# First head of the delta layer: key convolution in two halves, a hand-written inversion order, and the GpSimd remainders in four pieces

## The reference

```python
proj = hn @ w_in
qkv = jax.nn.silu(short_conv_centred(proj[..., :n_qkv], conv_w)).astype(f32)
gate = proj[..., n_qkv:n_qkv + B_VW].astype(f32)
ba = proj[..., n_qkv + B_VW:].astype(f32)
q = l2_norm(qkv[..., :B_KW].reshape(b, s, B_HEADS, B_HEAD_K))
...
beta = jax.nn.sigmoid(ba[..., :2 * B_HEADS]).reshape(b, s, 2, B_HEADS)
g = -jnp.exp(a_log.astype(f32)) * jax.nn.softplus(a + dt_bias.astype(f32))
o_fwd = gated_delta_chunked(q, k, v, g[:, :, 0], beta[:, :, 0])
o_bwd = flip(gated_delta_chunked(flip(q), flip(k), flip(v), flip(g[:, :, 1]), flip(beta[:, :, 1])))
...
# in gated_delta_chunked, per chunk and head:
lower = jnp.where(strict, jnp.einsum('bnhcd,bnhed->bnhce', kb, k) * decay, 0.0)
a_mat = jnp.eye(CHUNK, dtype=q.dtype) + lower
sol = lax.linalg.triangular_solve(a_mat, rhs, left_side=True, lower=True, unit_diagonal=True)
# then a scan over the chunks
```

## Time and profile before

| | |
|---|---|
| median of 3 runs | 1339.96 us (1338.75 to 1340.84) |
| profiled execution | 1342.17 us, span 1340.5 us |
| mean granted TensorE clock | 0.986 of full speed |
| busy: PE, PEld | 95%, 73% of the span |
| busy: DVE, ACT, POOL | 64%, 52%, 21% |
| chain that ended last | PE 75%, DVE 11%, ACT 9% |
| layer 0 and the passage to layer 1 | until about 517 us |
| first head's preparation and inversion | 517 to 628 us |

### The profile page before, as it was taken

One profiled execution on the slowest core, in us unless ns is written; L12 is line 12 of the kernel. 1 busy time (PEld: TensorE's weight loads), 2 busy tenths in 40 slices (PEclk: granted clock), 3 DMA queues, 4 the chain that ended last, 5 costly groups with the idle time before them and its releaser, 6 DMA issues.

```text
span 1340.5 us, 23647 instructions
## 1 busy us (share of the span) xinstructions
PE 1270.4 (95%) x8829; PEld 973.2 (73%) x8829; DVE 852.6 (64%) x2340; ACT 691.8 (52%) x1806; POOL 278.3 (21%) x188
## 2 busy tenths in 40 slices
PE   5999999999999999878999999999999999998997
PEld 4866766666667776667888888888888888865643
DVE  5334545444656545786897978879788797852343
ACT  6245465464564444535557485574856647552121
POOL 7220111020232244204104031040310403100000
PEclk9999999999999989888999999999999999999999
DMA  5111101011322231111011111110201101053111
GB/s 195 33 32 32 33 32 32 17 32 64 126 69 89 79 126 64 49 33 49 32 33 64 33 52 45 53 60 17 79 18 65 48 18 64 1 221 110 48 68 74
DMA packets 21761, 79.94 MB, mean 60 GB/s; under 512 B 3216, under 2 KB 3472, under 8 KB 20240
## 3 DMA queue, kind: packets, MB, share of 16 engines
q1 hardware_dynamic: 21648, 78.42, 17.0%
HBM read 63.66 MB, written 14.75 MB: 58 GB/s over the span
## 4 chain that ended last, share of the span: by engine, by line
PE 75%; DVE 11%; ACT 9%; issue 2%; DMA 2%; SPq 0%; POOL 0%; DVEq 0%; POOLq 0%
PE bank L1865 19%; PE bank L1765 17%; PE bank L1841 6%; PE bank L1905 4%; PE bank L1880 4%; PE bank L1792 4%; DVE arena L1504 3%; PE bank L1803 3%; PE bank L1818 3%; PE bank L1957 2%; PE bank L1964 2%; PE bank L1990 2%; PE bank L1938 2%; PE bank L1939 2%; PE bank L1950 2%
## 5 line engine op out<-in xcount | busy, mean ns | idle before, releaser
L1865 PE MATMUL bank<-hn_hi,w_hi 128*128 128x512 f32 x512 | 222.5, 435 | 0.5 <-ACT arena L1147 0.5
L1865 PE MATMUL bank<-hn_hi,w_lo 128*128 128x512 f32 x512 | 202.5, 395 | 0.0
L1865 PE MATMUL bank<-hn_lo,w_hi 128*128 128x512 f32 x512 | 201.4, 393 | 0.0
L1765 PE MATMUL bank<-hn_hi,w_hi 128*128 128x512 f32 x320 | 137.0, 428 | 0.5 <-ACT arena L1082 0.2
L1765 PE MATMUL bank<-hn_hi,w_lo 128*128 128x512 f32 x320 | 126.1, 394 | 0.0
L1765 PE MATMUL bank<-hn_lo,w_hi 128*128 128x512 f32 x320 | 125.8, 393 | 0.0
L1003 POOL TENSOR_TENSOR w_lo<-arena,w_hi 128x1024 fp32r<-128x1024 f32 x24 | 59.9, 2495 | 301.6 <-ACT w_hi L1178 301.6
L1113 ACT ACTIVATE arena<-bank 128x512 f32<-128x512 f32 x88 | 52.2, 598 | 118.0 <-PE bank L1803 118.0
L1865 PEld LDWEIGHTS bank<-hn_hi,w_lo 128*128 128x128 f32 x512 | 96.8, 189 | 22.1
L1363 DVE CUSTOM_DVE_ANT_0 arena<-bank,arena 128x384 f32<-128x384 f32 (+1 forms) x128 | 70.1, 581 | 63.7 <-issue 63.4
L1865 PEld LDWEIGHTS bank<-hn_hi,w_hi 128*128 128x128 f32 x512 | 97.6, 191 | 16.2 <-ACT arena L1147 0.7
(11 more groups left out here) (258 smaller groups left out, 2744.4 us busy)
## 6 DMA issues: line engine op xcount, KB each, us to landing
arena<-in_w SPq DMA_DIRECT2D x52, 512.0 KB, 3.5
arena<-in_x SPq DMA_DIRECT2D x16, 512.0 KB, 4.6
arena<-gc_scratch SPq DMA_DIRECT2D x8, 1024.0 KB, 4.8
x_scratch<-arena SPq DMA_DIRECT2D x13, 512.0 KB, 2.6
arena<-x_scratch SPq DMA_DIRECT2D x13, 512.0 KB, 3.5
out<-arena SPq DMA_DIRECT2D x8, 512.0 KB, 2.6
oT_scratch<-arena SPq DMA_DIRECT2D x7, 512.0 KB, 5.3
arena<-oT_scratch SPq DMA_DIRECT2D x7, 512.0 KB, 7.8
```

Of the source, the lines that this page charges most:

```text
L1765: ins = te.matmul(bank[r % 2][:], wp[:, tile % 2, k], hp[:, k, hf * HALF:(hf + 1) * HALF], start=(k == 0 and m == 0), stop=(k == KT - 1 an ...
L1865: ins = te.matmul(b[:], wp[:, t % 2, k], hp[:, k, hf * HALF:(hf + 1) * HALF], start=(k == 0 and m == 0), stop=(k == KT - 1 and m == 2))
```

## The change

The diff has six parts. (1) `first_inversion` replaces `inversion(0)`: the query's taps 0 and 1 before `x4`, 2 and 3 after `plain`, 4 after `y4`, then the value's five taps and SiLU (which stood before the inversion), then three taps of the next key, and its last two after `wqq`. (2) In front, eight items instead of four before the key's transposes, three instead of six before `subc`; one item more in all. (3) `lev` (level rows of the second direction, now with the zeroing of `invT`) stands right behind the first key's SiLU, not before `subc`; the zeroing left the place between the two copies of the gate logits. (4) The first key's half tiles are copied by ScalarE in front of and between its gate functions, and VectorE convolves tokens 0 to 509 before it builds its constants, the rest at the old place. (5) The second pair of the first head's four `subc` copies is VectorE's. (6) Every weight remainder at lines 955 and 1003 is made in four pieces of 256 columns; the semaphore rises after the last.

```diff
@@ -609,6 +609,39 @@
             def spread(h):
                 return [("init", h, rnd, p) for rnd in range(2) for p in range(2)] + [("turn", h)]
 
+            def first_inversion():
+
+                f(2)
+                conv("Q", 0, 0, 1)
+                f(1)
+                stage("x4", 0)
+                stage("plain", 0)
+                conv("Q", 0, 2, 3)
+                f(2)
+                stage("y4", 0)
+                conv("Q", 0, 4)
+                put(("silu", "Q", 0))
+                conv("V", 0, 0, 1, 2, 3, 4)
+                put(("silu", "V", 0))
+                f(2)
+                stage("x5", 0)
+                conv("K", 1, 0, 1, 2)
+                f(2)
+                put(("gramq", 0, 0), ("gramq", 0, 1))
+                stage("y5", 0)
+                put(("wqq", 0, 0, 0), ("wqq", 0, 0, 1), ("wqq", 0, 1, 0), ("wqq", 0, 1, 1))
+                conv("K", 1, 3, 4)
+                f(3)
+                stage("x6", 0)
+                f(2)
+                stage("y6", 0)
+                put(("root", 0))
+                f(2)
+                put(("vtr", 0, 0), ("vtr", 0, 1), ("silu", "K", 1))
+                f(4)
+                put(("tab1", 1), ("etm", 1, 0), ("etm", 1, 1))
+                f(3)
+
             def inversion(h):
                 prev, nxt = h - 1, h + 1
                 more = f if h < B_HEADS - 1 else fe
@@ -661,19 +694,17 @@
             put(("gcum",), ("gctr",))
             f(1)
             conv("K", 0, 0, 1, 2, 3, 4)
-            put(("silu", "K", 0), ("tab1", 0), ("etm", 0, 0), ("etm", 0, 1))
-            f(4)
+            put(("silu", "K", 0), ("lev",), ("tab1", 0), ("etm", 0, 0), ("etm", 0, 1))
+            f(8)
             put(("ktr", 0, 0), ("ktr", 0, 1), ("ssq", 0))
             f(4)
             put(("gramk", 0, 0), ("gramk", 0, 1), ("tabx", 0), ("ete", 0, 0), ("ete", 0, 1), ("stab", 0),
                 *[("wqk", 0, g, cc) for g in range(2) for cc in range(4)])
-            f(6)
-            put(("lev",), ("subc", 0, 0), ("subc", 0, 1), ("diag", 0, 0), ("diag", 0, 1), *sub_pieces(0))
+            f(3)
+            put(("subc", 0, 0), ("subc", 0, 1), ("diag", 0, 0), ("diag", 0, 1), *sub_pieces(0))
             f(25)
             put(*spread(0))
-            conv("V", 0, 0, 1, 2, 3, 4)
-            put(("silu", "V", 0))
-            inversion(0)
+            first_inversion()
             for h in range(1, B_HEADS):
 
                 sub = sub_pieces(h)
@@ -952,8 +983,11 @@
 
                     tile = e[1]
                     pool.wait_ge(w0_rounded, tile + 1)
-                    gp.tensor_tensor(w0_lo[:, tile % 2], ring0[:, tile % 2], w0_hi[:, tile % 2].bitcast(F32),
-                                     ALU.subtract).then_inc(w0_split, 1)
+                    for k in range(0, KT, 2):
+                        ks = slice(k, k + 2)
+                        ins = gp.tensor_tensor(w0_lo[:, tile % 2, ks], ring0[:, tile % 2, ks], w0_hi[:, tile % 2, ks].bitcast(F32),
+                                               ALU.subtract)
+                    ins.then_inc(w0_split, 1)
                 elif e[0] == "wosplit":
 
                     j = e[1]
@@ -1000,7 +1034,10 @@
                         continue
                     pool.wait_ge(w_rounded, t + 1)
                     pool.wait_ge(w_split, t)
-                    gp.tensor_tensor(w_lo[:, t % 2], ring1[:, t % 2], w_hi[:, t % 2].bitcast(F32), ALU.subtract).then_inc(w_split, 1)
+                    for k in range(0, KT, 2):
+                        ks = slice(k, k + 2)
+                        ins = gp.tensor_tensor(w_lo[:, t % 2, ks], ring1[:, t % 2, ks], w_hi[:, t % 2, ks].bitcast(F32), ALU.subtract)
+                    ins.then_inc(w_split, 1)
                 elif e[0] == "etm" and e[1] > 0:
 
                     h, d = e[1], e[2]
@@ -1117,6 +1154,14 @@
                     sc.activation(w_hi[:, i], ring1[:, i], ACT.Copy).then_inc(w_rounded, 1)
 
 
+            def first_key(hf):
+                e = ("proj", 0, hf, KT - 1)
+                act.wait_ge(W_full, W_DONE[w_key(e)])
+                sc.activation(raw[:, 0, 2 + hf * HALF:2 + (hf + 1) * HALF], w_bank(e)[:],
+                              ACT.Copy).then_inc(W_free[W_BANK[w_key(e)]], 1)
+
+            act.wait_ge(l1_ready, 1)
+            first_key(0)
             act.wait_ge(ba_tr, 1)
             act.wait_ge(ld_small, 16 * 7)
             bt = bank[4][:, 0:NT * 32].rearrange("p (c e) -> p c e", e=32)
@@ -1129,6 +1174,7 @@
             act.wait_ge(ba_dve, 2)
             sc.activation(gtmp[:, 2], gtmp[:, 2], ACT.Ln).then_inc(ba_act, 1)
             sc.activation(alb[:], alb[:], ACT.Exp).then_inc(ba_act, 1)
+            first_key(1)
             act.wait_ge(gc_copied, 1)
             sc.activation(gates[:, 2], gates[:, 1], ACT.Exp).then_inc(ba_act, 1)
 
@@ -1137,7 +1183,7 @@
                 return w_bank(e), W_free[W_BANK[w_key(e)]]
 
             for e in EV:
-                if e[0] == "proj" and e[3] == KT - 1:
+                if e[0] == "proj" and e[3] == KT - 1 and e[1] > 0:
                     part, h = TILES[e[1]]
                     hf = e[2]
                     b, fr = full(e)
@@ -1222,7 +1268,7 @@
                     for i in range(2):
                         act.wait_ge(*evicted(("proj", TILES.index(("G", h)), i, 0)))
                     sc.activation(gate_of(h), gate_of(h), ACT.Silu).then_inc(gate_done, 1)
-                elif e[0] == "subc":
+                elif e[0] == "subc" and e[1:] != (0, 1):
 
                     h, part = e[1:]
                     act.wait_ge(gk_done, h * 2 + 2)
@@ -1416,11 +1462,30 @@
                     for rnd in range(2):
                         link(ve.tensor_copy(inE[rows, rnd, d], bc(ident[rows, rows], 4)))
 
+            CUT = HALF - 2
+
+            def first_key_tap(j, lo, hi):
+
+                tap = cw[:, 5 * W1_PART["K"] + j:5 * W1_PART["K"] + j + 1]
+                dst, src = k_c[:, 0, lo:hi], raw[:, 0, lo + j:hi + j]
+                if j == 0:
+                    ins = ve.tensor_scalar(dst, src, tap, None, ALU.mult)
+                else:
+                    ins = ve.scalar_tensor_tensor(dst, src, tap, dst, ALU.mult, ALU.add)
+                if j == 4 and hi == SEQ:
+                    ins.then_inc(conv_done, 1)
+                else:
+                    link(ins)
+
             for hf in range(2):
                 dve.wait_ge(ba_full, hf + 1)
                 ve.tensor_copy(baT[:, hf * HALF:(hf + 1) * HALF], bank[2 + hf][0:32, :]).then_inc(ba_copied, 1)
                 if hf == 0:
 
+                    dve.wait_ge(*evicted(("proj", 0, 0, 0)))
+                    dve.wait_ge(consts, 3 + 3)
+                    for j in range(5):
+                        first_key_tap(j, 0, CUT)
                     dve.wait_ge(consts, 3 + 3 + 4 + 2)
                     part = vpp[:, 1, 0:1].bitcast(I32)
                     code, odd, pair = (vpp[:, 5, n:n + 1].bitcast(I32) for n in range(3))
@@ -1437,7 +1502,6 @@
                     link(ve.tensor_tensor(vpp[:, 2].bitcast(I32), iv, jv, ALU.bitwise_xor))
                     link(ve.tensor_scalar(vpp[:, 3].bitcast(I32), vpp[:, 2].bitcast(I32), LV0, None, ALU.logical_shift_right))
                     link(ve.tensor_scalar(vpp[:, 4], vpp[:, 3].bitcast(I32), 1.0, None, ALU.is_equal))
-                    ve.memset(invT, 0.0)
             dve.wait_ge(ba_act, 1)
             bt = bank[4][:, 0:NT * 32].rearrange("p (c e) -> p c e", e=32)
 
@@ -1482,6 +1546,7 @@
             for e in EV:
                 if e[0] == "lev":
                     level_rows(1)
+                    ve.memset(invT, 0.0)
                 elif e[0] == "etm" and e[1] == 0:
 
                     d = e[2]
@@ -1489,6 +1554,18 @@
                     link(ve.tensor_tensor(ET[:, d], ET[:, d], bc(emask[:, d], NT), ALU.add))
                     dve.wait_ge(tab_dve, 1)
                     ve.tensor_tensor(ET[:, d], ET[:, d], bc(head_tab2[:, 0, 2, NT * d:NT * d + NT], P, 2), ALU.add).then_inc(et_masked, 1)
+                elif e[0] == "subc" and e[1:] == (0, 1):
+
+                    dve.wait_ge(gk_done, 2)
+                    src = wq.rearrange("p d c t i -> p (d c) t i")[:, :, 0]
+                    for q in (2, 3):
+                        rows = slice(32 * q, 32 * q + 32)
+                        ins = ve.tensor_copy(sub_c[rows], src[rows, :, 32 * q:32 * q + 32])
+                    ins.then_inc(subc_done, 1)
+                elif e[:3] == ("conv", "K", 0):
+
+                    dve.wait_ge(*evicted(("proj", 0, 1, 0)))
+                    first_key_tap(e[3], CUT, SEQ)
                 elif e[0] == "conv":
 
                     part, h, j = e[1:]
```

## The result

| | before | after |
|---|---|---|
| median of 4 runs each, side by side | 1339.8 us | 1327.2 us (1326.1 to 1327.9) |
| span of the profiled execution | 1340.5 us | 1325.9 us |

The ratio is 0.9905, with a 95% interval of 0.9888 to 0.9922: 12.6 us or 0.95% faster, where 1326 (1318 to 1337) was forecast. The span shrank by 14.6 us.

The account below looks back on a forecast made before the run. TensorE, busy 95% of the span, bounds the kernel; only its idle stretches and slow work after them can be won. Terms +0.3 - 9.2 - 2 - 4 = -14.9, kept as -14, gave 1326 us (1318 to 1337).

Parts of the forecast that it names:

- The bound and the front's moments: TensorE 95% busy; idle before 622 us, mostly 529 to 622, can be won back; moments forecast up to value's transposes at 612.4.
- the new wait: Before head 0's level-5 inverse: TensorE idles 6.7 us for ScalarE's level-5 copies, queued behind the value's activation; ends at 600.6.
- Key in halves, four items, level rows: First key: convolution ends at 545.7, not 546.8; four items (2.8 us) already done; level rows' 2.1 us leave the later place.
- The block chain: Head 0 before level 4: one of two GpSimd subtractions leaves, the other costs 2.6 us; level-4 products 3.0 us earlier.
- The inversion: Head 0: no idle before level 4's second products, level-5 copies' wait goes; value's transposes at 612.4, 9.2 us earlier.
- Remainders in pieces, and the moved boundaries: Heads 1 to 6: recurrence up to -3.3 us, key taps 0 or +0.7 a head; -2 us for both.
- By that rule pieces cut the longest hold but not the sum: GpSimd remainders beside VectorE: whole instructions exclude each other; four pieces cost 2.8 us, 0.5 more than one subtraction.
- Rival 1: Only the front gains: boundaries cost 0.7 us in six heads, last loads no earlier; -5 us, 1335; chance 0.22.
- The start: First splits of layer 0 end about 1.3 us later; 0.3 us taken as the cost, between -0.3 and +1.3.
- The tail: Output-weight loads start 2.9 us earlier; the 2.80 us wait and its low clock go: 4 us, between 1 and 4.5.
- The sum: Whole kernel: +0.3 - 9.2 - 2 - 4 = -14.9, kept as -14; 1326 us.
- the reserve of 0.9: Whole kernel: -14 kept instead of -14.9, since several events lie within 0.1 us and a missed meeting costs.

Follow-up runs that it names:

- e6: The changed kernel with the four added projection items behind the first key's Gram products instead of ahead of its transposes; 1326.4 us.
- e4: The changed kernel with the first key's convolution in one piece in its old place; 1327.2 us.
- e10: The changed kernel with the level rows ahead of the block copies and the memset among the constants again; 1327.7 us.
- e9: The kernel before, with GpSimd's remainders in pieces and nothing else; 1338.1 us.
- e1: The changed kernel with each GpSimd remainder subtracted in one instruction again, in both layers; 1331.7 us.
- e2: The kernel before, with one projection item more (26 instead of 25) ahead of head 0's blocks; 1337.1 us.
- e8: The kernel before, with one item more ahead of head 0's blocks and GpSimd's remainders in pieces; 1329.7 us.
- e3: The changed kernel with head 0's old inversion: value taps and activation in front, old order inside; 1327.2 us.
- e5: The changed kernel with one item less (24 instead of 25) ahead of head 0's blocks; 1331.1 us.
- e13: The changed kernel with the value's activation behind the level-5 inverse's copies and three of the next key's taps behind them; 1319.5 us.

## Why the prediction was right, and where it was not

**The bound and the front's moments.** Right within about 1.5 us: turned logits 531.33 (forecast 531.4), level-4 products 578.93 (579.9), wait there 6.5 us (5.9), second products 583.88 with no wait (584.6), the new wait 6.15 us ending at 599.09 (6.7, 600.6), none over 0.4 us at the old line 2070 (2147 now), value's transposes 611.10 (612.4). So the front gave 10.5 us by its last moment instead of 9.2, or 8.9 with the 0.3 us of the start.

**Key in halves, four items, level rows.** The key's transposes start at 545.74 (547). As an account of gains this step was loose: it counted four items, 2.8 us, as already done. e6 shows that they are worth nothing where they stand. The halves are worth 1.3 us (e4), the level rows 1.3 (e10), the pieces 1.6 in the old kernel (e9) and 0.5 in the new one (e1), where halves under a remainder are short anyway. The sharing of the block copies was not run by itself.

**The block chain.** One of the two subtractions now falls under the key-product scalings, which keep their 0.34 us each, as forecast. The price of the other came out nearly right for a reason that I had not: I let one subtraction hold up VectorE by 2.6 us. Four pieces meet four small adds there, each about 0.5 us longer than alone (the first four lines, timeline of VectorE after), together 2.0; with whole remainders it is one add of 2.28 (last line, e1):

```profile
566.14 0.72 DVE L1726 TENSOR_TENSOR arena<-arena 128x15 f32<-128x15 f32 x1
566.89 0.68 DVE L1728 TENSOR_TENSOR arena<-arena 128x15 f32<-128x15 f32 x1
567.61 0.66 DVE L1726 TENSOR_TENSOR arena<-arena 128x28 f32<-128x28 f32 x1
568.30 0.65 DVE L1728 TENSOR_TENSOR arena<-arena 128x28 f32<-128x28 f32 x1
...
567.33 2.28 DVE L1722 TENSOR_TENSOR arena<-arena 128x28 f32<-128x28 f32 x1
```

**The inversion.** The moments were right and the credit was wrong. (The terms for the value's taps add up to 596.6, not 596.7, which changes nothing; the activation started at 595.20.) I gave all 9.2 us to the halves, the chain and the new order. Of the 6.5 us in B the item alone gives 3.5 (e2), item and pieces 5.4 (e8), both with the front's other edits 5.9 (e3), and the new order adds the last 0.6, no more than the clock moves B by itself. I had asked what the item does to the later heads and to the tail, not to head 0, where the earlier trace rows shows the tile copy at 602.73 that it moves.

**Remainders in pieces, and the moved boundaries.** "By that rule pieces cut the longest hold but not the sum" is the step that failed. I counted two pieces, 1.4 us, against 1.32 us of slack and got 0; a whole remainder I didn't price at this place. Two pieces do meet the taps, as counted, but at 0.35 us each and not 0.7: they cost VectorE 0.71 us, a whole one 1.98. Pieces cut the sum for two reasons: the last two of them slip behind the taps, and each meeting costs less than the piece's own length. At the moved boundary they are worth 5 us over the heads (e1). With the pieces in, C is 1.06 us shorter, not 2: the seven waits in the recurrence went, but line 2130 waits 0.35 us in each head, line 2147 some 0.35 and line 2015 0.25, 0.95 together, where it was 0.5 and 0.8 before. That is 2.3 us less idle time in C, but TensorE is also busy 1.3 us longer there (488.27 instead of 486.99 us, with the same 4539 products at a granted clock of 1.00); why is open. Rival 1 said that all hung on a small difference, and e1 and e2 show its case: 0.8 us a head.

The Trainium skill, SBUF — State Buffer, Who interferes with whom, says that the shared port pair is an exclusive lock, and that issue order decides who blocks. The small adds and the three taps in 5.90 us agree, and so does the turn-taking above: a piece issued during a tap goes before the next tap. The hold seen here is shorter than the instruction, by the 0.4 us above.

**The start.** Over all executions the first projection products of layer 0 start at 28.1 to 28.6 us with whole remainders and at 28.1 to 29.2 with pieces, 0.5 us later in the mean (forecast 0.3). It is lost in the scatter of layer 0's end.

**The tail.** -3.12 us instead of -4. The loads were released 2.9 us earlier, as forecast, but the wait did not go (TensorE's timeline after, and, in the second line, of e5, where the item is taken away):

```profile
1179.23 2.81 PE L1957 MATMUL bank<-arena 128*128 128x512 f32 x6 [1.37 <-DMA arena<-oT_scratch]
...
1181.12 2.38 PE L1957 MATMUL bank<-arena 128*128 128x512 f32 x3 [3.62 <-DMA arena<-oT_scratch]
```

Measured from the last head's level-4 products the output products start 1.4 us earlier (16.65 instead of 18.08), since the first `oT_scratch` load took 9.0 us from issue to use instead of 7.5. The other 1.7 us are the clock: six products take 2.81 us instead of 4.51, and the mean granted clock in D is 1.00 instead of 0.83. The idle stretch ahead of them is 1.37 us long instead of 2.80; in the eleven executions where it is 1.4 us or shorter they take 2.81, in the three where it is 2.8 or longer 4.3 to 4.5. The forecast priced the release and not the transfer.

**The sum** came out within 1.2 us (1326 against 1327.2) because the misses had both signs: the front gave 1.6 us more, heads and tail 1.8 less, and the reserve of 0.9 was my choice. That the total is close is therefore luck in part.

## What to carry to other kernels

A remainder on GpSimd is worth cutting where it falls beside long VectorE instructions with two SBUF inputs, and does nothing beside PSUM copies and next to nothing beside a chain of short ones. An edit that shifts a stream of fillers by one moves every copy and rounding that hangs on it, in the first head too: read the order of the in-order engines around each moved boundary, with and without the other edits, since their effects don't add. Before filling one wait, look at the next one: if a chain on another engine sets its end, the filling is free and also worthless, and what stands ahead of the critical copies in ScalarE's queue is where the time lies (here 5 to 6 us).

## What was not expected of the hardware

- Four GpSimd pieces beside VectorE taps took 5.32 us instead of 2.82, and up to 6.80 (e4), since each waits out a whole tap, while a tap loses only 0.35 us to a piece that lasts 0.72 alone. Why the hold is 0.4 us shorter than the instruction is open.
- After the 2.7 us wait in the tail, four output products took 3.46 us after the change, 1.98 or 1.99 in five other executions (e1, e5, e9, e10, e13) and 2.67 to 3.78 in the other eight, with hardly another wait before them. The granted clock over the next 3.5 us is 1.00 in the five and between 0.50 and 0.67 in the rest. The Trainium skill, TensorE: Matmul & The Clock Gate, Part 1, says of the products at the start of a kernel that the number of slow ones is run-variable. The same is seen here behind an idle stretch in the middle of one, by 1.5 us, with no edit near. The two of e5 and after:

```profile
1199.38 1.98 PE L1957 MATMUL bank<-arena 128*128 128x512 f32 x4 [2.61 <-DVE arena L1679]
...
1195.98 3.46 PE L1957 MATMUL bank<-arena 128*128 128x512 f32 x4 [2.66 <-DVE arena L1679]
```
